# A new order for a hybrid decoder layer on eight cores: VectorE and GpSimd planned apart, the first norm ahead of the role branch, and the halves divided at column 2256

## The reference

```
h = RMSNorm(x); [u_pool | u_rnn | u_gate | g_pool | g_rnn] = h @ W_in         (1024 -> 4608)
y_pool = (trailing means of u_pool over 2, 4, 8, 16 tokens, less the token, @ per-group maps) @ W_pool_out
v      = causal conv of 4 taps over u_rnn;  r, i = sigmoid(block-diagonal maps of v)   (8 heads of 128)
a_t    = sigmoid(lam)^(8 r_t);  s_t = a_t s_(t-1) + sqrt(1 - a_t^2) i_t v_t            (a scan over tokens)
y_rnn  = (s * gelu(u_gate)) @ W_rnn_out
x = x + (sigmoid(g_pool) y_pool + sigmoid(g_rnn) y_rnn) @ W_o
x = x + (silu(gate) * up) @ W_ffn_out, with [gate | up] = RMSNorm(x) @ W_ffn_in         (2 x 2816)
out = RMSNorm(x)
```

## Time and profile before

| what | us |
|---|---|
| median of 3 executions | 1068.47 |
| lowest and highest of them | 1067.85, 1217.47 |
| the profiled execution, its own time | 1069.25 |
| its span (first to last instruction of the slowest core, core 7, role b) | 1067.6 |
| spans of role a (cores 0, 2, 4, 6) | 1017.3, 1021.8, 1016.5, 1017.5 |
| spans of role b (cores 1, 3, 5, 7) | 1067.4, 1066.8, 1066.5, 1067.6 |

### The profile page before, as it was taken

How to read it: one execution, slowest core, us unless ns; L and a number is a source line. 1 busy time by engine, 2 the same in 40 slices (tenths; PEclk the granted TensorE clock), 3 DMA queues, 4 the chain that set the end, 5 groups by cost and what they waited for, 6 DMA issues and landing times.

```text
span 1067.6 us, 13774 instructions; the slowest of 8 cores (1016.5 to 1067.6 us)
## 1 busy us (share of the span) xinstructions
PE 932.8 (87%) x4484; PEld 447.6 (42%) x4484; DVE 596.9 (56%) x745; ACT 535.6 (50%) x767; POOL 410.3 (38%) x421
## 2 busy tenths in 40 slices
PE   3293477688699899998999999999999999999995
PEld 2041133233234444443444444455544455555552
DVE  1278898999998855786533434543334343221225
ACT  2477678788678742567656457722223261111112
POOL 1338973866788448553201103341044310010000
PEclk9596689899999999999999999999999999999998
DMA  9524550024253038973432205683253599128003
GB/s 186 121 76 140 145 102 1 13 48 96 40 90 69 11 90 217 190 110 66 76 54 40 40 1 97 145 156 60 38 134 64 102 216 230 20 37 181 1 1 139
DMA packets 42765, 97.15 MB, mean 91 GB/s; under 512 B 3776, under 2 KB 21312, under 8 KB 42560
## 3 DMA queue, kind: packets, MB, share of 16 engines
q0 software_dynamic: 23904, 63.45, 34.4%
q1 hardware_dynamic: 18784, 32.74, 9.9%
HBM read 151.88 MB, written 7.73 MB: 150 GB/s over the span
## 4 chain that ended last, share of the span: by engine, by line
PE 75%; issue 8%; DVE 7%; POOL 5%; ACT 3%; ACTq 0%; DVEq 0%; POOLq 0%
PE bank L655 71%; PE bank L624 3%; PE bank L701 2%; POOL q L727 2%; DVE h L635 1%; DVE wi L730 1%; DVE wi L714 1%; DVE v L692 1%; POOL vb L697 1%; POOL keep_hst L733 1%; POOL sq L599 1%; DVE pA L769 1%; ACT q L724 1%; DVE pl L784 0%; ACT L724 0%
## 5 line engine op out<-in xcount | busy, mean ns | idle before, releaser
L655 PE MATMUL bank<-h,wf 128*128 128x452 bf16 (+3 forms) x1408 | 286.0, 362 | 0.0
L655 PEld LDWEIGHTS bank<-h,wf 128*128 128x128 bf16 x1408 | 137.0, 97 | 144.5 <-issue 1.6
L692 DVE SCALAR_TENSOR_TENSOR v<-bank,keep_cst,v 128x488 f32<-128x488 f32 (+4 forms) x200 | 128.5, 683 | 41.7 <-POOL v L689 29.4
L655 PE MATMUL bank<-h,wu 128*128 128x492 bf16 (+5 forms) x576 | 130.1, 378 | 22.6 <-DVE h L635 11.3
L655 PE MATMUL bank<-ff,wz 128*128 128x492 bf16 (+3 forms) x704 | 142.8, 362 | 0.0
L945 DVE TENSOR_TENSOR ff<-tf,bank 128x492 bf16<-128x492 f32 (+3 forms) x88 | 56.3, 642 | 137.8 <-PE bank L655 119.4
L940 ACT ACTIVATE tf<-bank 128x492 f32<-128x492 f32 (+3 forms) x88 | 49.2, 564 | 126.3 <-PE bank L655 125.5
L655 PEld LDWEIGHTS bank<-ff,wz 128*128 128x128 bf16 x704 | 68.9, 98 | 71.7 <-issue 1.4
L613 ACT ACTIVATE sq<-x 128x492 f32<-128x492 f32 (+3 forms) x56 | 33.0, 595 | 127.7 <-DVE x L957 104.6
L655 PEld LDWEIGHTS bank<-h,wu 128*128 128x128 bf16 x576 | 58.2, 102 | 88.9 <-issue 38.6
L697 POOL CAST vb<-v 128x488 bf16<-128x488 f32 (+4 forms) x72 | 63.6, 889 | 76.0 <-DVE v L692 63.4
(11 more groups left out here) (96 smaller groups left out, 1340.5 us busy)
## 6 DMA issues: line engine op xcount, KB each, us to landing
wf<-wfi POOLq DMA_DIRECT2D x44, 512.0 KB, 8.7
wz<-wfo POOLq DMA_DIRECT2D x16, 704.0 KB, 9.1
xt<-xT SPq DMA_DIRECT2D x16, 492.0 KB, 6.7
wu<-w_in POOLq DMA_DIRECT2D x16, 256.0 KB, 11.2
wg<-w_in POOLq DMA_DIRECT2D x16, 256.0 KB, 5.7
wb<-w_in POOLq DMA_DIRECT2D x16, 256.0 KB, 7.7
wa<-w_in POOLq DMA_DIRECT2D x16, 256.0 KB, 8.0
wr<-wro POOLq DMA_DIRECT2D x16, 256.0 KB, 6.5
```

The costliest lines, as they stand in the source:

```text
L655: last = e.matmul(p.tensor[:, 0:n], lhsT=wap(kc), rhs=rhs(kc), start=(kc == 0), stop=(kc == K - 1))
L692: g.op("dve", c_dve(w), k, lambda e, p=p, o=o, w=w, s=s: e.scalar_tensor_tensor(out=v.tensor[:, o:o + w], in0=p.tensor[:, HALO - s:HALO - ...
```

## The change

1. `XS` becomes 2256. Role a's tiles are 256, 416, 400 and 344, 508, 332; role b's own tiles 476, 480 and 440, 444, its prefix tiles 256 and four times 500. The number of tiles, and so of matmul instructions, stays.
2. The planner gets a `port`: operations of DVE and POOL that touch SBUF alone are marked, and a marked one lasts until the marked one before it, on either engine, is over. In role b an operation whose port is taken is also ranked lower (`port_pen`). The assumed POOL durations change a little.
3. The one-column POOL copy of the scan's state goes. The next group's scan reads its initial value straight from the last column of the previous result; where the buffer cannot be kept (the last prefix group, the first chunk) ACT copies it.
4. In role b's second chunk (`ps=1`) the second gate stays in its PSUM bank: DVE does the two multiplications and the scan per tile against the bank, and the scan writes into `v`.
5. The cast of `v` may go to ACT (role a, second chunk, three heads).
6. The head now holds the DVE constants, squares, statistics and rsqrt of the first norm, four `wu` loads and `rg`. The first `wu` load names the third piece of `x` as read, so that POOL's queue waits for its landing. PE, ACT and DVE read the role before the head and branch after it.
7. All keys are new, and some choices of engine: role a adds the two halves of the merge (`mx`) on DVE instead of POOL; role b's second chunk has taps for six heads on POOL instead of eight, and `mx` on POOL instead of DVE.

```diff
-XS = 2208
+XS = 2256
...
 def c_pool(n):
-    return 0.06 + 0.0022 * n
+    return 0.09 + 0.00228 * n
...
+                    if o.port and port > t:
+                        pen += prm["port_pen"] * (port - t)
...
+                if o.port:
+                    dur += max(0.0, port - t)
+                    port = t + dur
...
+        head += [g.op("dve", 0.2, K, lambda e: e.memset(ones.tensor[:], 1.0 / D), wr=[ones]),
...
+        acc = self.squares(self.xt0, W0 + HALO, K, "pe", "act", "n1")
+        self.rstd0 = self.stat(acc, W0 + HALO, K, "n1")
+        head += g.ops[n:]
+        self.wu0 = []
+        for j in range(4):
+            b = self.buf("wu", [8, 128], BF16)
+            rd = [self.xt0[2]] if j == 0 else []
+            head.append(g.op("pool", 0.58, K, lambda e, b=b, j=j: e.dma_start(out=b.tensor[:], in_=dr["w_in"][4 + j]), rd=rd, wr=[b],
+                             nbytes=128 * 1024 * 4, tag="wu"))
...
+        if ps:
+            pieces = []
...
+            hid = v
+        else:
+            pieces = [(0, W, lambda: wi.tensor[:], allp(wi), allp(v))]
+            hid = wi
+        for o, w, x, xk, vk in pieces:
...
+            prev = (None if first else self.state[j]) if o == 0 else (lambda o=o: hid.tensor[:, o - 1:o], hk)
...
-        g.op("pool", 0.15, k + 2, lambda e: e.tensor_copy(out=self.hst.tensor[:, j:j + 1], in_=wi.tensor[:, W - 1:W]),
-             rd=allp(wi), wr=[(self.hst, j)], tag="hc")
+        if save:
+            g.op("act", 0.18, k + 2, lambda e: e.activation(out=self.hst.tensor[:, j:j + 1], in_=hid.tensor[:, W - 1:W], func=AF.Copy),
+                 rd=allp(hid), wr=[(self.hst, j)], tag="hc")
+            self.state[j] = (lambda: self.hst.tensor[:, j:j + 1], [(self.hst, j)])
+        else:
+            self.state[j] = (lambda: hid.tensor[:, W - 1:W], allp(hid))
...
-            emit(e, name, plans["a"], 0, n)
-            v = e.value_load(role_d[0:1, 0:1])
+            if name in ("sp", "pool"):
+                emit(e, name, plans["a"], 0, n)
+                v = e.value_load(role_d[0:1, 0:1])
+            else:
+                v = e.value_load(role_d[0:1, 0:1])
+                emit(e, name, plans["a"], 0, n)
```

More of the change, by code:

```diff
@@ L59 @@
     __slots__ = ("eng", "dur", "key", "fn", "deps", "bufs", "table", "nbytes", "idx", "tag", "est", "nwait",
-                 "start", "end", "needs", "succ", "sem", "val", "know", "sig", "alloc", "late")
+                 "start", "end", "port", "succ", "sem", "val", "know", "sig", "alloc")
     def __init__(self, eng, dur, key, fn):
@@ L69, in __init__ @@
         self.start = self.end = None
-        self.needs = True
+        self.port = False
         self.succ = []
@@ L83, in __init__, with op @@
         self.readers = {}
-    def op(self, eng, dur, key, fn, rd=(), wr=(), table=None, nbytes=0, tag="", late=0.0):
+    def op(self, eng, dur, key, fn, rd=(), wr=(), table=None, nbytes=0, tag="", port=False):
         o = Op(eng, dur, key, fn)
@@ L89, in op @@
         o.tag = tag
-        o.late = late
+        o.port = port
         o.idx = len(self.ops)
@@ L300, in run @@
         left = len(ops)
-        at = {e: 1.0 for e in ENGINES}
-        self.fixed = [b for o in head for b in o.bufs]
+        self.head = head
+        at = dict(prm["at"])
+        port = 0.0
+        self.fixed = []
         for o in head:
+            self.fixed += [b for b in o.bufs if b.space == "sb" and b.left is None]
             ready[o.eng].remove(o)
             self.do_alloc(o, 0.0)
[L306 to L309, removed]
+            o.start = max([at[o.eng]] + [d.end + prm["lag"] for d in o.deps])
+            dur = o.dur
+            if o.eng == "act" and o.table is not None and (table is None or table not in o.table):
+                table = o.table[0]
+                dur += 1.35
+            at[o.eng] = o.start + dur
+            o.end = o.start + dur
+            if o.nbytes:
+                dma_free = max(o.end, dma_free) + o.nbytes / prm["dma_rate"]
+                o.end = dma_free + prm["dma_lat"]
             self.order[o.eng].append(o)
@@ L420, in signals @@
                 n += 1
+        for o in self.head:
+            o.sig = not o.nbytes
         for o in seq:
@@ L632, in norm, with apply @@
              rd=[ln], wr=[pss], table=EXPL, tag=tag + "rs")
+        return pss
+    def apply(self, pss, S, parts, w, gcol, out, key, tag):
+        g, cst = self.g, self.cst
         for kc in range(8):
@@ L807, in build @@
         if pre:
-            wus = self.wu0 + [self.weight("wu", [8, 128], dr["w_in"][4 + j], P["rnn"][0][0] + P["rnn"][0][1] * j) for j in range(2, 8)]
+            wus = self.wu0 + [self.weight("wu", [8, 128], dr["w_in"][4 + j], P["rnn"][0][0] + P["rnn"][0][1] * j) for j in range(4, 8)]
             i = 0
@@ L859, in chunk @@
             self.rnn_group(j, [(h, w, i) for i, (h, w) in enumerate(tw)], wu[j], key("rnn", j), kk["rnn"][2], first, G[j],
[L860 removed]
+                           ("act" if j < kk["sq_act"] else "pool", "pool" if j < kk["mul_pool"] else "dve", j >= 8 - kk["tap"], "act" if j < kk["vb_act"] else "pool", kk["ps"]), not last)
         PL = []
@@ L989 @@
         ]),
     b=dict(
-        begin=dict(pe=6.0, act=6.0, dve=6.0, pool=9.0, sp=4.0), window=88.58, table_pen=36.88, dma_rate=185000.0, dma_lat=2.2,
-        lag=0.08, pe_lag=0.5, bank_lag=0.05, lead=5.7, xlead=28.41, reserve=26818.0, near=16.84, cap=199105.0,
-        prefix=[256, 488, 488, 488, 488], groups=[2, 2, 1], own=[[492, 496], [448, 452]], wp=74.72, window2=93.4,
-        pre=dict(n=[83.76, -136.85, 175.35, 232.92, 222.76], n_on='pool',
-             rnn=[[-82.44654614519426, 2.4, 2.61], [226.86, 0.14, 27.54], [18.23, 10.17, 5.16]], sq_act=0, mul_pool=6,
-             tap=0, ns_on='act'),
@@ new lines @@
+        dma_lat=2.2, lag=0.08, pe_lag=0.5, bank_lag=0.05, lead=15.77, xlead=47.17, reserve=20232.0, near=13.4, cap=194672.0,
+        prefix=[256, 500, 500, 500, 500], groups=[2, 2, 1], own=[[476, 480], [440, 444]], wp=-98.71, window2=76.33,
+        at=dict(pe=4.0, act=2.5, dve=1.0, pool=1.5, sp=1.0), jump=dict(pe=5.5, act=5.5, dve=5.5, pool=5.5, sp=5.5),
+        port_pen=12.07,
+        pre=dict(n=[-271.03, -78.18, -93.92, 14.75, -194.37], n_on='pool',
+             rnn=[[-289.05, 0.45, 14.78], [120.76, 2.3, 35.56], [-203.0653055637369, 12.16, 26.6]], sq_act=0, mul_pool=6,
+             tap=0, ns_on='act', vb_act=0, ps=0),
```

179 lines of the change are left out of this document (108 added, 71 removed).

## The result

The changed kernel takes 1056.97 us (median of 4, 1053.99 to 1059.60), the kernel before 1069.66 beside it; the ratio is 0.9878, 95% interval [0.9842, 0.9913]. Measured again in another job, beside some of the experiments, the same kernel took 1046.28, ratio 0.9781 [0.9743, 0.9820]. Forecast were 1036, 3% less than before, and a range of 1025 to 1051: the first measurement lies 6 us outside it, the second inside. Some executions of either kernel run some per cent longer with one die's cores at a lower granted clock; they are left out of the ratios and of the ranges and medians of cores.

What follows compares the result with a forecast made beforehand. PE bounds role a and role b after 374 us, DVE role b before. Role a: +20.5 - 5, taken as 1035.2; role b: 1067.6 - 15.5 - 26 - 6 = 1020.1. The later plus 0.85 gives 1036 us, range 1025 to 1051.

Steps and rivals of the forecast that it cites:

- Which role ends last: After the change role a, at 1035.2 us, ends later than role b, at 1020.1; chance 0.60 that role a sets the time.
- Part 1: Division moved to 2256: role a 20.5 us longer, role b 15.5 us shorter in its PE-bound part.
- I cost this at nothing: Role b's stretch before 374 us: 48 prefix columns come in, 32 own leave, 3 us either way.
- Parts 5 and 7: Engine moves where PE is never idle, including casts on ACT: no effect, queues carrying as many DMAs as before.
- Parts 2, 3 and 6 in role b: Port-aware planning and dropped one-column copies gain 26 us, mainly before 374 us; the reordered head gains 6.
- one order-dependent stall after another: Such stalls filled 79 us of role b's PE idle time; argued for role b still setting the time, chance 0.27.
- DVE is its bound: Role b from 60 to 374 us: DVE, busy 282 of 314 us, limits the stretch.
- Part 6, the head: Earlier first norm at the start: role a gains 5 us (-3 to 9.5), role b 6 (0 to 9).
- Part 4: Second gate kept in PSUM, role b's second chunk: no effect since PE sets the pace; 6 us without that cover.
- The slower rival: Role b's second chunk runs out of PSUM banks, up to 128 us of standing PE; 1090 us, chance 0.03.
- What was to show each step: Signs: last square before 11 us, projection near 17, scans 2.33 us, 500-column product 0.65, role a's PE unbroken after 200.

Runs made afterwards that it cites:

- run 4: Changed kernel with the division back at 2208 and the old tile widths, new code and keys kept: 1062.37 us, ratio 0.9921.
- fenced: Changed kernel with one wait more in role a, a wf load waiting for the 508-column tile's x loads: 1037.17 us, ratio 0.9688.
- run 3: Kernel before with only the division at 2256 and the new tile widths, old keys and code: 1066.53 us, ratio 0.9963.
- run 2: Changed kernel measured once more in another job, nothing edited: 1046.28 us, ratio 0.9781.
- run 5: Kernel before with the 40 one-column copies moved from POOL to DVE, right behind their scans: 1064.64 us, ratio 0.994.
- run 6: Fenced kernel with port_pen 0 instead of 12.07 in role b: 1057.45 us, ratio 0.9865; control with port_pen 24: 1036.88 and 1038.10 us.
- run 8: Fenced kernel, three starts: no wu wait for x 1046.48 us; SP's x behind the branch waiting for four wu 1044.26; rg behind four wu 1040.32.
- run 7: Fenced kernel with ps=0 in role b's second chunk, its second gate back in SBUF: 1037.71 us, ratio 0.968.

## Why the prediction was wrong, step by step

*Which role ends last*: right. *Part 1*, +20.5 in role a: of the right size. It came to 16 us between the same keys at the two divisions (medians of 1010 in run 4 and 1026 fenced), and with the old keys to 27, 6 of them idle time. Role b's -15.5 in the PE-bound part agrees with the rows but was not measured by itself; "I cost this at nothing" for the stretch before it failed with the old keys, by the one wait of 21.9 us (run 3).

*Parts 5 and 7, "nothing either, and SP's and POOL's queues carry as many DMAs as before"*: this is the step that failed. It counted the DMAs and not how the two queues stand to each other. The new order let eleven `wf` loads go 9 us ahead of the `x` load that the plan had in front of them; PE then stood 14 to 16 us, and role a became 18 us longer than with that one order restored. The step did not put the result outside the range alone. With the stall and the clock at 1.00 the kernel took 1046, inside it (run 2); the low clock of one die in the first measurement, 10 to 12 us, came on top, and it belongs to no step of the prediction. With the order restored the kernel is at 1037.17, where 1036 was forecast. That these two agree is luck: role a, forecast at 1035, is then at 1026, and role b, forecast at 1020, sets the time with 1035. A rival "a transfer is overtaken" was not among mine.

*Parts 2, 3 and 6 in role b, 26 and 6 us*: too large, and by the wrong mechanism. By medians on its chip role b of the fenced kernel is 32 us shorter than before; less the 15.5 of the columns, 17 are left of 32. The forecast took 26 of the 32 from stretched DVE and POOL instructions. DVE's busy time between 60 and 374 fell by 10 us, of 36 that were stretched, and the scans stayed as slow. Who PE waited for in that stretch tells more. Here is the longest entry of core 7 in the kernel before, then in the changed one (us in total, times, longest):

```profile
PE bank L624 <- ACT sq L584: 28.3, 2, 28.1
```
```profile
PE bank L697 <- DVE h L674: 16.5, 3, 8.5
```

Before, 28.1 of PE's 79 idle us were one single wait, for ACT's squares of a first norm. It is nearly the same with the copies moved (27.0, run 5), and it is gone in the changed kernel, whose PE idles 59 us. My list of costs has no such term: "one order-dependent stall after another" was only said of the rival. "DVE is its bound" was half of the truth, since an order of the queues that removes one wait is worth as much as shorter DVE work. How the 17 us divide between this wait, the ranking (20 us if it is taken away, run 6), the copies (7 us in the old order, run 5) and the head was not settled; the effects do not add.

*Part 6, the head*: role a, 5 us: the first 200 us have 11 us more PE work on core 4 than core 0 had before, and at the old division role a is 9 us shorter by medians, so the size was about right or too small. Role b, 6 us: the norm came 7 us earlier (13.5 instead of 20.5), the first projection 4 (20.0 instead of 24.0), since it then waited for `wu`, and after 60 us PE was 3 us behind, not ahead. But without the wait in the head role b is 8 us longer (run 8). So the wait is worth 8 in the new order; what the rest of the head gives was not separated.

*Part 4*: nothing, right (run 7). *The slower rival* found no support.

*What was to show each step*: on core 0 the last square ended at 8.9 and the first projection began at 17.8, no copy is left on POOL, and the 500-column product takes 674 ns, as forecast. The 1000-column scans at 3.10 us instead of 2.33, and the 16 us of idle PE in role a after 200 us, are the two signs that failed.

In run 5 a one-column copy took 154 ns on DVE, where the earlier trace rows have 872 for it on POOL among DVE's two-input instructions. The rule of the Trainium skill on this (page "SBUF — State Buffer", section "SBUF: two separate sides": whichever of a GpSimd operation and such a DVE operation starts first has the shared ports for its whole length, and the other waits) agrees with that. The 2.80 us of POOL in the earlier trace rows are two squares back to back (x2 in that row), and the DVE operation was held through both. Of the time of the kernel the collisions decided little as far as is shown: those of the scans stayed, and the gain came all the same.

## What to carry to other kernels

A plan that fixes the order of each queue does not fix the order between queues: where a planner gives one load priority by time alone, look in the trace for big prefetches on another queue that are issued ahead of it, and let the first of them wait for the small urgent load. When an order is redrawn, list for each needed load what bytes are in flight at its issue; 5.8 MB of weights and 2.1 MB of `x` at 215 GB/s are 37 us. Look at the longest single waits of the engine that sets the time before working out shares of busy time: one of 28 us was a third of PE's idle time here. And effects of a division and of an order are not to be added: 4 and 8 us alone were 32 together.

## What the runs showed of the hardware that was not expected

With the DMA full at 210 to 222 GB/s, four loads of together 2 MB from the SP queue took 27 us from the last one's issue, behind 5.8 MB (11 MB in HBM) issued 2 to 14 us earlier on POOL's queue; the median from issue to landing was 21 us, and 5.8 us without these. The queues shared the DMA meanwhile: between 710 and 720 us SP's moved 0.79 MB and POOL's 1.54. The clock granted to TensorE had a mean of 0.58 over the 20 us with the stall, was at 0.50 (1.2 GHz) for some 5 us after it, and was at 1.00 in the same stretch without it. And in one measurement the cores of one die had a mean of 0.97 over 300 us of nearly unbroken PE work, made up of 1.00 and stretches of 4 to 8 us at 0.81, where the other die, and both dies in another measurement of the same kernel, had 1.00.
